# A decoder block on one core: the output projection's tiles in another order, and the pooling mixer divided between GpSimd and VectorE

## The reference, cut to what matters

```python
h = rms_norm(x, pre_mix_g)
q, k, v, u_pool, u_conv, g_logits = split(h @ w_in)
attn = moba_attention(q, k, v, rel_bias) @ w_attn_o        # 8 heads of 64
pool = pool_mixer(u_pool, w_pool_g, pool_scale) @ w_pool_o
conv = conv_module(u_conv, ...) @ w_conv_o                  # depthwise, 31 taps
merged = sum_i sigmoid(g_logits_i + b_gate_i) * (attn, pool, conv)[i]
x = x + rms_norm(merged @ w_out, post_mix_g)
h = rms_norm(x, pre_ffn_g)
x = x + rms_norm((silu(h @ w_gate) * (h @ w_up)) @ w_ffn_out, post_ffn_g)
```

## Time and profile before

| what | value |
|---|---|
| median of the runs | 744.56 us (744.15 to 746.15) |
| the profiled execution's own time | 747.17 us |
| its span in the trace | 745.4 us |
| TensorE (PE) busy | 725.5 us, 97% |
| VectorE (DVE), ScalarE (ACT), GpSimd (POOL) busy | 387.8, 270.4, 62.3 us |
| mean granted clock of TensorE | 0.996 |
| DMA | 75.6 MB, mean 101 GB/s |

### The profile page before, as it was taken

How to read it: one execution, slowest core, us unless ns; L and a number is a source line. 1 busy time by engine, 2 the same in 40 slices (tenths; PEclk the granted TensorE clock), 3 DMA queues, 4 the chain that set the end, 5 groups by cost and what they waited for, 6 DMA issues and landing times.

```text
span 745.4 us, 9259 instructions
## 1 busy us (share of the span) xinstructions
PE 725.5 (97%) x3362; PEld 604.8 (81%) x3362; DVE 387.8 (52%) x579; ACT 270.4 (36%) x430; POOL 62.3 (8%) x73
## 2 busy tenths in 40 slices
PE   5999999999999999998999999999999999999996
PEld 4787788888888888886898888888888888888885
DVE  5448778578576556894545434343443433123124
ACT  6323544544546463243424232232323222123211
POOL 2004600000000002740100000000000000000001
PEclk9999999999999999999999999999999999999999
DMA  7342232232231314238114332323333232332303
GB/s 237 115 141 58 86 113 84 84 113 84 84 113 56 114 57 141 85 115 253 57 29 142 93 105 85 113 85 94 103 91 106 84 112 85 102 96 91 108 28 113
DMA packets 110456, 75.60 MB, mean 101 GB/s; under 512 B 2995, under 2 KB 99251, under 8 KB 110428
## 3 DMA queue, kind: packets, MB, share of 16 engines
q1 hardware_dynamic: 110412, 75.20, 33.4%
q10 hardware_dynamic: 16, 0.02, 0.0%
HBM read 73.10 MB, written 2.12 MB: 101 GB/s over the span
## 4 chain that ended last, share of the span: by engine, by line
PE 92%; DVE 3%; DMA 1%; issue 1%; ACT 1%; POOL 0%; DVEq 0%; POOLq 0%; ACTq 0%
PE bank L1044 29%; PE bank L1045 29%; PE bank L1046 29%; PE bank L1095 1%; DMA raw<-in_w_out_dram 1%; DVE wo_lo L673 1%; PE bank L1062 1%; PE bank L1112 1%; PE bank L1085 1%; PE bank L1111 1%; PE bank L1086 1%; DVE mix L918 0%; DVE conv_acc L738 0%; DMA x_tok<-in_x_dram 0%; PE bank L1239 0%
## 5 line engine op out<-in xcount | busy, mean ns | idle before, releaser
L1044 PE MATMUL bank<-h_hi,w_hi 128*128 128x512 f32 (+1 forms) x712 | 274.0, 385 | 1.8 <-DVE h_lo L701 1.8
L1046 PE MATMUL bank<-h_hi,w_lo 128*128 128x512 f32 (+1 forms) x712 | 272.1, 382 | 0.0
L1045 PE MATMUL bank<-h_lo,w_hi 128*128 128x512 f32 (+1 forms) x712 | 272.0, 382 | 0.0
L673 DVE TENSOR_TENSOR w_lo<-raw,w_hi 128x1024 fp32r<-128x1024 f32 x116 | 147.6, 1273 | 149.5 <-ACT w_hi L406 139.8
L406 ACT ACTIVATE w_hi<-raw 128x1024 fp32r<-128x1024 f32 x108 | 113.9, 1055 | 162.6 <-PE bank L1046 162.4
L1044 PEld LDWEIGHTS bank<-h_hi,w_hi 128*128 128x128 f32 x712 | 133.9, 188 | 27.4 <-issue 2.2
L1046 PEld LDWEIGHTS bank<-h_hi,w_lo 128*128 128x128 f32 x712 | 133.8, 188 | 26.4
L1045 PEld LDWEIGHTS bank<-h_lo,w_hi 128*128 128x128 f32 x712 | 133.9, 188 | 24.8
L1044 PE MATMUL bank<-w_hi,f_hi 128*128 128x512 f32 x176 | 68.5, 389 | 0.0
L1045 PE MATMUL bank<-w_lo,f_hi 128*128 128x512 f32 x176 | 68.5, 389 | 0.0
L1046 PE MATMUL bank<-w_hi,f_lo 128*128 128x512 f32 x176 | 68.5, 389 | 0.0
(11 more groups left out here) (155 smaller groups left out, 656.5 us busy)
## 6 DMA issues: line engine op xcount, KB each, us to landing
raw<-in_w_ffn_in_dram SPq DMA_DIRECT2D x44, 512.0 KB, 3.8
raw<-in_w_in_dram SPq DMA_DIRECT2D x42, 512.0 KB, 3.9
raw<-in_w_ffn_out_dram SPq DMA_DIRECT2D x22, 512.0 KB, 3.8
raw<-in_w_branch_dram SPq DMA_DIRECT2D x8, 512.0 KB, 3.6
raw<-in_w_out_dram SPq DMA_DIRECT2D x8, 512.0 KB, 3.8
x_tok<-in_x_dram SPq DMA_DIRECT2D x4, 512.0 KB, 5.0
bias_h<-bias_scratch SPq DMA_DIRECT2D x4, 512.0 KB, 5.2
x<-in_x_dram SPq DMA_DIRECT2D x2, 1024.0 KB, 7.8
```

What stands on the lines that cost most here:

```text
L673: dve.tensor_tensor(dst, src_hi[0], src_hi[1], ALU.subtract).then_inc(lo_done, 1)
L1044: pe.matmul(dst, a_hi, b_hi, start=start, stop=False)
L1045: pe.matmul(dst, a_hi, b_lo, start=False, stop=False)
L1046: return pe.matmul(dst, a_lo, b_hi, start=False, stop=stop)
```

## The change

It has two parts in one kernel.

**Pooling mixer.** GpSimd keeps the window sums alone. It no longer waits for `s_full`; the first two additions are done for each half on its own, the first half as soon as it is copied (`acc_act` at 3), so there are six additions (the last two as before). The correction of the first 16 tokens, the factor 1/w and the subtraction are now `pool_diff` on VectorE: for each of two groups of 64 rows one multiplication of 64x32 and two scalar_tensor_tensor of 64x512. Pair 0 is written out on VectorE (the loop has two passes, 1 and 2): its taps stand in units 1, 2, 3, 7 and 8, and `pool_diff` in units 4 and 5.

**Output projection.** The tiles' order becomes (0,2), (1,0), (1,1), (0,3), turn 0, (1,2), turn 1, (1,3); turn 2 and turn 3 stand behind the first and the second half unit of the feed-forward. On ScalarE and VectorE the splits of the turned tiles stand earlier in the order.

```diff
@@ GpSimd
-            pool.wait_ge(pads_done, 2)
-            pool.wait_ge(acc_act, 4)
-            pool.wait_ge(s_full, 2)
-            link(pool.tensor_tensor(sum_a[:, :, 1:n], u_pool[:, :, 1:n], u_pool[:, :, 0:n - 1], ALU.add))
-            link(pool.tensor_tensor(sum_b[:, :, 3:n], sum_a[:, :, 3:n], sum_a[:, :, 1:n - 2], ALU.add))
+            pool.wait_ge(pads_done, 2)
+            for c in range(2):
+                pool.wait_ge(acc_act, 3 + c)
+                link(pool.tensor_tensor(sum_a[:, c, 1:n], u_pool[:, c, 1:n], u_pool[:, c, 0:n - 1], ALU.add))
+                link(pool.tensor_tensor(sum_b[:, c, 3:n], sum_a[:, c, 3:n], sum_a[:, c, 1:n - 2], ALU.add))
             link(pool.tensor_tensor(sum_a[:, 1, 7:n], sum_b[:, 1, 7:n], sum_b[:, 1, 3:n - 4], ALU.add))
-            link(pool.tensor_tensor(sum_b[64:P, 1, 15:n], sum_a[64:P, 1, 15:n], sum_a[64:P, 1, 7:n - 8], ALU.add))
...
+            pool.tensor_tensor(sum_b[64:P, 1, 15:n], sum_a[64:P, 1, 15:n], sum_a[64:P, 1, 7:n - 8], ALU.add)\
+                .then_inc(sums_done, 1)
@@ VectorE
+            def pool_diff(part):
+                lo_row, s_ = ((0, sum_a), (64, sum_b))[part]
+                rows = slice(lo_row, lo_row + 64)
...
+                if part == 0:
+                    dve.wait_ge(sums_done, 1)
+                dve.tensor_tensor(s_[rows, :, POOL_PAD:POOL_PAD + 16], s_[rows, :, POOL_PAD:POOL_PAD + 16],
+                                  ratio[rows, :, :], ALU.mult).then_inc(sums_scaled, 1)
+                dve.wait_ge(sums_scaled, part + 1)
+                for c in range(2):
+                    ins = dve.scalar_tensor_tensor(out=d_pool[rows, c, :], in0=s_[rows, c, POOL_PAD:],
+                                                   scalar=const[rows, C_INV + c:C_INV + c + 1],
+                                                   in1=u_pool[rows, c, POOL_PAD:], op0=ALU.mult, op1=ALU.subtract)
+                ins.then_inc(d_done, 1)
...
+                    elif first:
+                        if j in (1, 2, 3, 7, 8):
+                            taps(p, {1: 0, 2: 2, 3: 4, 7: 6, 8: 8}[j])
+                        if j in (4, 5):
+                            pool_diff(j - 4)
...
-            with dve.Fori(0, PAIRS - 1) as p:
+            pair_steps(0, False, first=True)
+            with dve.Fori(1, PAIRS - 1) as p:
@@ ScalarE
+            sq_y(0); sq_x(0); hi_int(U_FF)
+            sq_y(1); sq_x(1); hi_int(U_FF + 1); h2_hi_part(0)
+            sq_y(2); h2_hi_part(1); sq_x(2); hi_int(U_FF + 2)
+            sq_y(3); sq_x(3); h2_hi_part(2); h2_hi_part(3)
@@ VectorE
+            residual(0); norm_x1(0); lo_int(U_FF)
+            residual(1); norm_x1(1); lo_int(U_FF + 1); h2_lo_part(0)
+            residual(2); h2_lo_part(1); norm_x1(2); lo_int(U_FF + 2)
+            residual(3); norm_x1(3); h2_lo_part(2); h2_lo_part(3)
@@ TensorE
+            out_tile(0, 0, range(6, 8)).then_inc(d0_full, 1)
+            out_tile(0, 1, range(6, 8)).then_inc(d0_full, 1)
+            pe.wait_ge(mix_read, KT)
+            out_tile(0, 2, range(KT)).then_inc(d0_full, 1)
+            out_tile(1, 0, range(KT)).then_inc(d1_full, 1)
+            out_tile(1, 1, range(KT)).then_inc(d1_full, 1)
+            out_tile(0, 3, range(KT)).then_inc(d0_full, 1)
+            turn_x1(0)
+            out_tile(1, 2, range(KT)).then_inc(d1_full, 1)
+            turn_x1(1)
+            out_tile(1, 3, range(KT)).then_inc(d1_full, 1)
...
-                    if n == 0 and e == 2:
-                        turn_x1(3)
+                    if n == 0 and e:
+                        turn_x1(e + 1)
```

More of the change, by code:

```diff
@@ L188, in build @@
             sem("br_split"), sem("br_mm"), sem("br_act"), sem("br_ready"))
+        sums_done, sums_scaled = sem("sums_done"), sem("sums_scaled")
         mix_read, mix_part, mix_sum, m_hi, m_lo = sem("mix_read"), sem("mix_part"), sem("mix_sum"), sem("m_hi"), sem("m_lo")
@@ L346, in link @@
                 pool.wait_ge(pool_tick, tick)
-            link(pool.tensor_tensor(sum_a[:, :, 1:n], u_pool[:, :, 1:n], u_pool[:, :, 0:n - 1], ALU.add))
-            link(pool.tensor_tensor(sum_b[:, :, 3:n], sum_a[:, :, 3:n], sum_a[:, :, 1:n - 2], ALU.add))
-            link(pool.tensor_tensor(sum_a[:, 1, 7:n], sum_b[:, 1, 7:n], sum_b[:, 1, 3:n - 4], ALU.add))
-            link(pool.tensor_tensor(sum_b[64:P, 1, 15:n], sum_a[64:P, 1, 15:n], sum_a[64:P, 1, 7:n - 8], ALU.add))
[L352 to L362, removed]
+            pool.wait_ge(pads_done, 2)
[3 more added lines that the diff above has]
+                link(pool.tensor_tensor(sum_b[:, c, 3:n], sum_a[:, c, 3:n], sum_a[:, c, 1:n - 2], ALU.add))
+            link(pool.tensor_tensor(sum_a[:, 1, 7:n], sum_b[:, 1, 7:n], sum_b[:, 1, 3:n - 4], ALU.add))
+            pool.tensor_tensor(sum_b[64:P, 1, 15:n], sum_a[64:P, 1, 15:n], sum_a[64:P, 1, 7:n - 8], ALU.add)\
+                .then_inc(sums_done, 1)
             pool.wait_ge(ln_dve, 5)
@@ L617, in h2_hi_part @@
                                    bank[b][:, :].rearrange("p (k c) -> p k c", c=P), ACT.Copy).then_inc(h2_hi, 1)
[L619 to L626, removed]
+            sq_y(0)
+            sq_x(0)
+            hi_int(U_FF)
+            sq_y(1)
+            sq_x(1)
+            hi_int(U_FF + 1)
+            h2_hi_part(0)
+            sq_y(2)
+            h2_hi_part(1)
+            sq_x(2)
+            hi_int(U_FF + 2)
+            sq_y(3)
+            sq_x(3)
+            h2_hi_part(2)
+            h2_hi_part(3)
             def f_hi_part(j, b):
@@ L790, in o_lo_part, with pair_steps @@
                    .then_inc(vo_read, 1)
-            def pair_steps(p, last):
+            def pool_diff(part):
+                lo_row, s_ = ((0, sum_a), (64, sum_b))[part]
+                rows = slice(lo_row, lo_row + 64)
+                ratio = const[:, C_RATIO:C_RATIO + 32].rearrange("p (c t) -> p c t", c=2)
+                if part == 0:
[8 more added lines that the diff above has]
+                ins.then_inc(d_done, 1)
+            def pair_steps(p, last, first=False):
                 for j in range(PAIR_UNITS):
@@ L965, in h2_lo_part @@
                        .then_inc(h2_lo, 1)
[L967 to L974, removed]
+            residual(0)
+            norm_x1(0)
+            lo_int(U_FF)
+            residual(1)
+            norm_x1(1)
+            lo_int(U_FF + 1)
+            h2_lo_part(0)
+            residual(2)
+            h2_lo_part(1)
+            norm_x1(2)
+            lo_int(U_FF + 2)
+            residual(3)
+            norm_x1(3)
+            h2_lo_part(2)
+            h2_lo_part(3)
             def f_lo_part(j, b):
```

## The result

The changed kernel takes 740.14 us, the median of 6 runs (739.84 to 741.48), beside 744.94 us for the kernel before in the same set (6 runs, 744.15 to 746.15). The ratio is 0.9935 with a 95% interval of 0.9924 to 0.9945: 4.8 us faster. Forecast were 7.9 us and 736.7. The sign was right, the size was not.

The account below looks back on a forecast made before the run. TensorE, busy 725.5 of 745.4 us, was taken as the bound. Pair 0's 3.3 us plus the output projection's 4.6 gave 7.9, from the median 744.56 to 736.7 us; own range 735.4 to 738.2, chance 0.74.

Parts of the forecast that it names:

- Steps 1 to 4: Pooling mixer, pair 0: earlier sums, moved taps and `pool_diff` cost TensorE nothing; its waits go, gaining 3.3 us.
- a crowded unit 3: Rival: VectorE has too much in unit 3 or 4 of pair 0; gain only 5.2 us, 739.4; chance 0.07.
- a cause other than GpSimd: Rival: pair 0's slow taps belong to the loops' first pass; the first part gives nothing, 740.0 us; chance 0.05.
- The rival of code that has to be fetched: VectorE's written-out pair 0 and loop passes may need code fetches; two uncovered give back 5.4 us, 742.1; chance 0.03.
- Step 7: Feed-forward entry: `h2_lo` of tile 1 is ready at 33.0 us, asked for at 34.4, so 1.4 to spare.
- the stretch loses 4.6 us: Output projection: six tiles and two turns take 39.0 us against 34.4 undisturbed; the new order gains 4.6 us.
- The slow matmuls behind the wait: Output projection: nearly all the loss beyond the wait, with granted clock 0.60 in the mean of 346 to 350 us.
- The wait itself: Output projection: TensorE's wait for the last block of `wo_lo`, about 2.5 of the 4.6 us lost.
- the whole offset of 2.6: The profiled execution, 747.17 us, stands 2.6 above the median of 744.56; taken off to state the forecast as a median.
- Step 6: Output projection: `xn` of tile 3 comes 0.2 to 0.3 us late, as before the change, costing nothing new.
- The slow rival: Ahead of the feed-forward, `h2_lo(1)` queued behind a whole tile's chain, 8.5 us late: 747.3 us; chance 0.03.
- bounds of -0.3 and +1.6: Bounds of the two parts' gains around the forecast, combined with a run-to-run difference of 1 us for its own range.

Follow-up runs that it names:

- e7: The kernel before with only GpSimd's wait for two scores (`s_full`) taken away: 747.63 us, ratio 1.0025.
- e8: The changed kernel with GpSimd's wait for two scores (`s_full`) put back: 743.07 us, ratio 0.9959 to the kernel before.
- e3: The kernel before with only the second part, the edits to the output projection: 744.38 us, ratio 0.9980.
- e5: The changed kernel with VectorE's `w_lo` of the third feed-forward unit moved from ahead of `residual(3)` to behind it: 739.42 us, ratio 0.9911 to the kernel before.
- e4: The changed kernel once more, no edit: 740.23 us, ratio 0.9926 to the kernel before.
- e1: The kernel before once more, no edit: 745.25 us, ratio 0.9991.

## Why the prediction was wrong

**Step by step.** Steps 1 to 4 were right. The additions ran from 45.3 to 56.3 us (57 expected), the third call of taps pushed the next `w_lo` back by 0.4 (8.35 us behind the first score matmul, 7.92 in pair 1 before; 0.6 expected), `pool_diff` took 1.6 us (1.7 taken) and was hidden, and pair 0 lost its 3.3 us. Over executions without a fall the first part alone is worth 3.24; over all of them 4.1, since the falls of pair 0 went too, which the prediction had not priced. The rivals of a crowded unit 3 and of a cause other than GpSimd fall, the latter by e7 and e8. The stretched taps and `w_lo` of e7 and e8 read two tensors in SBUF; with the rule of the Trainium skill (SBUF — State Buffer, "Who interferes with whom") on such operations, these rows agree. But `prob`, which reads one, was stretched as well: 2.12 us in place of 0.82 in before, 0.80 in place of 0.55 in e8. The collision is wider than the taps and `w_lo` to which the prediction put it down. The rival of code that has to be fetched fell: no wait of TensorE stands at a turn of VectorE's loop. Whether code was fetched in VectorE's idle time isn't shown. Step 7 was right: the first half unit began at once, 34.43 us after the start, 34.4 expected.

**The step that failed is the price of the second part**, "the stretch loses 4.6 us", carried into the sum as a gain of 4.6. It was read from one execution and is a property of that execution in two of its terms:

- *The slow matmuls behind the wait*, some 1.7 us. I took them for a consequence of this wait and wrote that what makes the clock fall goes with it. About half of all executions of before have such a fall, for 1.7 us, but not in one place, and the share doesn't hang on this wait: with the wait gone and all else as before (e3) it is still 6 of 12. It is the first part, without the waits of pair 0, that made falls rare.
- *The wait itself.* It was 2.3 us in that profile and 1.3, 1.9 and 1.9 in three others.

Both show in the projection's length: 58.26 in the profile used, 55.91 in the mean of the three others. That is 2.35 us of the 3.1 that the forecast had too many. And they are what stood that profile 2.2 us above its median: outside the two lengths its own time is 628.8 us, and that of the three others 628.9 to 629.1. I subtracted the whole gain from the profile's own time and then the whole offset of 2.6 to come to the median, and so counted the same 2.3 us twice. The offset was a warning; it had to be placed in the trace before it was taken off.

- *Step 6* made up the rest. It put `xn` of tile 3 at 6.9 us after (1,3) "for each tile", and looked at TensorE's side alone. On VectorE, (1,3) now ends only 6.3 us behind (1,2), since (0,3) no longer lies between them; `xn` of tile 2 ends at 370.5, and a `w_lo` and two gained copies stand behind it. The sum of tile 3 came 0.7 us late, the wait was 0.9 and not 0.2 us, and e5 gives these 0.7 back.

3.3 + 4.6 - 2.35 - 0.74 = 4.8, the measured gain. That it closes to the tenth is in part luck. How many executions of a set have a fall moves its median: in the set of e4, with 12 of 23 executions of before of the lower kind, the medians lie 5.3 us apart (745.56 against 740.23), and without falls it is 4.9. The slow rival didn't come: the list of waits has none for `h2_lo`.

The prediction's own range has a slip too: bounds of -0.3 and +1.6 with 1 us between runs give 735.4 to 739.3, not to 738.2. The measured 740.1 lies above either.

## What to carry to other kernels

Place the difference between a profiled execution and its median before summing against it: a loss that is in the profile but not in every execution counts only by the share of executions that have it. A wait for a DMA and a fallen clock behind a wait are such losses. Three or four profiles of one kernel show their spread, and counting the mean clock over all timed executions, with and without each edit, shows which edit makes the falls rarer; the place of a fall in one profile does not. When an order is changed, redo the queue of each engine behind the new bound, not only the latency of one chain; and when a collision is moved, look at what it meets in its new place.

## What was not expected of the hardware

- After a wait of TensorE the granted clock falls in some executions and in others not: not behind waits of 1.3, 1.9 and 1.9 us in the projection of three executions of before, but behind one of 2.3 in a fourth; behind those of pair 0 in e3 and not in e1; behind the wait of 1.8 us for `h_lo` near the start, which every profile has, in e4 alone. A fall costs 1.7 us. Whether a kernel has many or few is not chance alone: 50 of 111 executions with the waits of pair 0, 3 of 29 without them.
- GpSimd's tiny operations stretch too: this addition of one column (L366) takes 0.77 us in the changed kernel, while VectorE runs a `w_lo` (370.40 to 371.62), and in e5, where that `w_lo` is elsewhere, 0.19.

```profile
370.90 0.77 POOL L366 TENSOR_TENSOR stat<-stat 128x1 f32<-128x1 f32 x1 [1.74 <-ACT junk L407]
```

```profile
369.94 0.19 POOL L366 TENSOR_TENSOR stat<-stat 128x1 f32<-128x1 f32 x1 [1.75 <-ACT junk L407]
```
